# Masks for the diagonal blocks added by GpSimd instead of TensorE, no semaphore-clearing blocks between stages, and down-projection weights asked for earlier

## The reference

```python
z = rmsnorm(x) @ w_in                              # q, k, v, forget of group A; q, k, v of group B
# group A ("fox"), causal over the whole prompt; C = cumsum(log_sigmoid(forget))
s = q @ k.T * SCALE + (C[t] - C[s]); s = where(pos_s <= pos_t, s, -inf); o = softmax(s) @ v
# group B ("band"): own chunk of 64 and the 8 before it, with a learned bias by distance
# both groups once more for the streams, against their caches
x = x + rmsnorm(concat(rmsnorm(oA), rmsnorm(oB)) @ w_out)
h = rmsnorm(x)
x = x + rmsnorm((silu(h @ w_gate) * (h @ w_up)) @ w_down)
```

## Time and profile before

| what | value |
|---|---|
| median of 3 runs | 3088.11 us (3088.1 to 3093.4) |
| the profiled execution | 3088.66 us, span 3086.9 us |
| PE busy, share of the span | 2900.5 us, 94% |
| DVE, ACT, POOL busy | 1629.0, 1187.3, 631.5 us |
| mean granted TensorE clock | 0.977 of full speed |
| `attend` in the span | about 610 to 1325 us, its fox jobs to about 1005 |
| `mix_out`, `feed_forward` | from 1328.6 us, from 1591.7 us |
| last gate/up unit ends | about 2546.5 us |

### The profile page before, as it was taken

One profiled execution on the slowest core, in us unless ns is written; L12 is line 12 of the kernel. 1 busy time (PEld: TensorE's weight loads), 2 busy tenths in 40 slices (PEclk: granted clock), 3 DMA queues, 4 the chain that ended last, 5 costly groups with the idle time before them and its releaser, 6 DMA issues. The chain is left out here.

```text
span 3086.9 us, 57152 instructions
## 1 busy us (share of the span) xinstructions
PE 2900.5 (94%) x23073; PEld 2611.0 (85%) x23073; DVE 1629.0 (53%) x3168; ACT 1187.3 (38%) x2097; POOL 631.5 (20%) x544
## 2 busy tenths in 40 slices
PE   7999999889999889979959999999999998999998
PEld 7999999877778666758749999999999996887887
DVE  6222122176667567744456766776676663224443
ACT  5330000067767566644433334333433332223221
POOL 0000000032022123001134534453434330000000
PEclk9999999989999999989979999999999998999999
DMA  5322212142211886445623232333232425335553
GB/s 167 95 75 73 74 63 74 65 139 79 67 29 55 273 290 216 144 161 164 199 72 138 99 111 93 136 107 112 93 106 98 143 94 167 94 94 161 170 166 121
DMA packets 276157, 376.37 MB, mean 122 GB/s; under 512 B 16488, under 2 KB 203896, under 8 KB 263864
## 3 DMA queue, kind: packets, MB, share of 16 engines
q1 hardware_dynamic: 275608, 371.42, 37.5%
q10 hardware_dynamic: 288, 1.31, 0.1%
HBM read 283.52 MB, written 89.15 MB: 121 GB/s over the span
## 5 line engine op out<-in xcount | busy, mean ns | idle before, releaser
L1179 ACT ACTIVATE att_pts<-att_pt 128x384 f32<-128x384 f32 (+3 forms) x472 | 209.9, 483 | 224.0 <-PE att_pt L1065 209.5
L1168 ACT ACTIVATE att_sx<-att_sx,att_nm 128x640 f32<-128x640 f32 (+17 forms) x272 | 264.9, 980 | 9.4 <-DVE att_nm L1295 9.4
L79 PE MATMUL frt_pz<-frt_xhi,frt_hi 128*128 128x448 f32 (+1 forms) x640 | 230.5, 360 | 0.0
L81 PE MATMUL frt_pz<-frt_xhi,frt_lo 128*128 128x448 f32 (+1 forms) x640 | 230.5, 360 | 0.0
L80 PE MATMUL frt_pz<-frt_xlo,frt_hi 128*128 128x448 f32 (+1 forms) x640 | 230.0, 359 | 0.0
L514 DVE TENSOR_TENSOR frt_shared<-frt_pz,frt_rb 128x448 f32<-128x448 f32 (+1 forms) x80 | 48.9, 611 | 313.5 <-PE frt_pz L81 313.5
L1101 PE MATMUL att_po<-att_pts,att_vv 128*64 128x128 f32 x3296 | 212.1, 276 | 0.2 <-issue 0.2
L1065 PEld LDWEIGHTS att_pt<-att_eye,att_sx 64*128 64x128 f32 x3296 | 128.4, 139 | 98.5 <-ACT att_pts L1179 56.2
L1065 PE MATMUL att_pt<-att_eye,att_sx 64*128 64x64 f32 x3296 | 165.7, 232 | 46.1 <-ACT att_pts L1179 22.6
L1101 PEld LDWEIGHTS att_po<-att_pts,att_vv 128*64 128x64 f32 x3296 | 184.6, 138 | 11.3 <-ACT att_pts L1179 8.2
L79 PE MATMUL frt_pv<-frt_hi,frt_xhi 128*128 128x256 f32 (+1 forms) x544 | 157.4, 289 | 18.4 <-DVE frt_lo L446 15.5
(11 more groups left out here) (296 smaller groups left out, 8140.5 us busy)
## 6 DMA issues: line engine op xcount, KB each, us to landing
ahead_first<-mid_act SPq DMA_DIRECT2D x68, 704.0 KB, 6.7
ahead_second<-in_w_gu SPq DMA_DIRECT2D x33, 1024.0 KB, 5.1
ffn_wr<-in_w_gu SPq DMA_DIRECT2D x33, 1024.0 KB, 5.1
att_raw<-out_zT SPq DMA_DIRECT2D x64, 256.0 KB, 3.6
att_bb<-in_cache_ak SPq DMA_DIRECT2D x16, 1024.0 KB, 9.4
att_bb<-in_cache_av SPq DMA_DIRECT2D x16, 1024.0 KB, 10.0
mid_act<-ffn_ao SPq DMA_DIRECT2D x44, 362.0 KB, 2.4
out_zT<-frt_shared SPq DMA_DIRECT2D x64, 224.0 KB, 1.9
```

The source lines that it names most:

```text
L79: nc.tensor.matmul(out, a_hi(k), b_hi(k), start=(k == 0), stop=False)
L81: last = nc.tensor.matmul(out, a_lo(k), b_hi(k), start=False, stop=(k == kk - 1))
L1168: nc.scalar.activation(sx[n % NSX][:, e, :w], sx[n % NSX][:, e, :w], ACT.Exp, bias=nm[n % NSX][:, e:e + 1], scale=-1.0, accum_out=sums[n % ...
L1179: nc.scalar.activation(pts[G % NPT][:, :, 0:k, 64 * x:64 * x + 64], pt[x][:].rearrange("p (e j q) -> p e j q", e=2, q=64)[:, :, 0:k, :], A ...
```

## The change

1. **Mask.** The four matmuls on the diagonal and their operands go. `mask` (128 x 128) is made once. For each fox job POOL makes a masked copy of the bias of the last group: one TENSOR_TENSOR for the diagonal tile of both heads, and one COPY for the up to three tiles before it. It lies in a free part of `sx` or, from block 12 on, in a new buffer `mb`. DVE waits for it (`s_mk`) before the last group, and reads it instead of `bb`. POOL makes it three jobs ahead, for blocks 13 to 15 once DVE has evicted the job before. The stream masks move behind job 0's step in POOL's program, the band table to step 14.
2. **Start of attention.** The bias and the values of the first four tiles are asked for ahead of raw piece 2, the rest of both behind it.
3. **Clearing.** `mix_out` gets semaphores of its own, those of `feed_forward` are cleared by POOL within `mix_out`, behind its constants. Both clearing blocks go.
4. **Last gate/up unit.** Down blocks 8 to 11 are asked for a unit earlier, 12 to 15, the activations of tile 1, and 16 and 17 within the last unit. ACT splits the activations of tile 0 before the first eviction, and blocks up to 12 between evictions (6 before). DVE makes the low parts up to 10.

```diff
+                def masked(n):
+                    kind, p, i = JOBS[n]
...
+                    if 4 <= i < 12:
+                        pool.wait_ge(s_bi, 2 * S0[n - 2])
+                    if n == 12:
+                        pool.wait_ge(s_dc, 1)
+                    if i > 12:
+                        pool.wait_ge(s_bi, 2 * S0[n])
+                    nc.gpsimd.tensor_tensor(out[:, :, w - P:], bb[u][:, :, i * P:(i + 1) * P],
+                                            mask[:, None, :].to_broadcast([P, 2, P]), ALU.add).then_inc(s_mk, 1)
+                    if w > P:
+                        nc.gpsimd.tensor_copy(out[:, :, 0:w - P], bb[u][:, :, c0:c0 + w - P]).then_inc(s_mk, 1)
...
+                for n in range(3):
+                    masked(n)
                 for n in range(NJOB):
+                    if n == 1:
+                        stream_masks()
+                    if n == 14:
+                        band_table()
...
+                    if n + 3 < WIDE:
+                        masked(n + 3)
                     for x in splits_at(n):
                         split(x)
...
-                    if diag:
-                        for x in range(2):
-                            for e in range(2):
-                                r = slice(64 * e, 64 * e + 64)
-                                last = nc.tensor.matmul(S[e][k % 2][:, w - P:w], below[r, x, :], above[r, x, :], start=False,
-                                                        stop=(x == 1), skip_group_check=True)
...
+                    diag = fox(p) and tiles[-1] == i
+                    if diag:
+                        dve.wait_ge(s_mk, M0[n + 1])
                     for e in range(2):
-                        if fox(p):
+                        if diag:
+                            bias = masked_bias(n)[:, e, :]
+                        elif fox(p):
...
-                dve.wait_ge(s_pool, 8)
-                nc.vector.tensor_copy(below[:], ones[:])
-                nc.vector.tensor_copy(above[:], negs[:])
...
-                for x in range(NRAW):
+                for x in range(2):
                     load_raw(x)
-                load_bias(0)
-                load_v(0)
+                load_first(0, 4 * P, s_b0, s_v0)
+                for x in range(2, NRAW):
+                    load_raw(x)
+                load_first(4 * P, SEQ, s_b[0], s_v[0])
...
-        m.clear_sems()
         with nc.Block() as block:
...
+                for sem in later:
+                    pool.sem_clear(sem)
...
                     if n == NU - 2:
                         for q in range(4, 8):
                             down_weights(q)
-                    if n == NU - 1:
                         for sem in (l6, l3, l0):
                             sp.wait_ge(sem, NU - 1)
                         sp.wait_ge(s_t, 4 * (NU - 1))
                         for q in range(8, 12):
                             down_weights(q)
+                    if n == NU - 1:
+                        for q in range(12, 16):
+                            down_weights(q)
+                        acts(1)
+                        for q in range(16, 18):
+                            down_weights(q)
```

More of the change, by code:

```diff
@@ L661, in attend @@
     E0 = counted(1 if is_stream(n) else 2 for n in range(NJOB))
+    M0 = counted(min(len(job_groups(n)[-1]), 2) for n in range(NJOB) if JOBS[n][0] == "fox")
     ORDER = attend_order()
@@ L710, in attend @@
         eye = m.sb("eye", [P, P])
[L711 to L714, removed]
+        mask = m.sb("mask", [P, P])
+        mb = m.sb("mb", [P, 2, 4 * P])
         mine = m.sb("mine", [P, P])
@@ L1011, in score @@
                     q = slice(i * P, (i + 1) * P)
-                    diag = fox(p) and tiles[-1] == i
                     if p == 0 and i % 4 == 0:
@@ L1729, with up_sems, down_sems, feed_forward @@
 FFN_BYTES = AT_AO + 16 * max(w for _, w in TWIN)
-def feed_forward(nc, t, keep, ahead):
+def up_sems(m):
+    st = [m.sem(f"a_stored{u}") for u in range(2)]
+    l_w = [m.sem(f"weights{u}") for u in range(2)]
+    h0, ht, h3, h6, l0, lt, l3, l6 = (m.sem(f"w_{a}_{b}") for a in ("high", "low") for b in ("first", "sums", "lower", "up"))
+    (l_h, s_t, s_sp, s_sd, s_hh, s_hl, s_pr, s_p1, s_add, s_g1, s_g2, s_a) = (m.sem(n) for n in (
+        "h", "w_sums", "h_sums_pool", "h_sums_dve", "h_high", "h_low", "products", "first", "added",
+        "silu1", "silu2", "act"))
+    return (st, l_w, h0, ht, h3, h6, l0, lt, l3, l6, l_h, s_t, s_sp, s_sd, s_hh, s_hl, s_pr, s_p1, s_add, s_g1, s_g2, s_a)
+def down_sems(m):
+    l_d = [m.sem(f"down_weights{u}") for u in range(8)]
+    s_first = m.sem("first_high")
+    s_low = m.sem("a_low_pool")
+    l_x = [m.sem(f"x1{u}") for u in range(2)]
+    st_y = [m.sem(f"y_stored{u}") for u in range(2)]
+    (l_a, s_g, s_wh, s_wl, s_used, s_ah, s_al, s_y, s_ev, s_ss, s_vv, s_rr, s_sc, s_out, s_pw) = (m.sem(n) for n in (
+        "act_in", "gain", "down_high", "down_low", "down_used", "a_high", "a_low", "down_products", "evicted", "squares", "var", "rms",
+        "scaled", "out", "power"))
+    return (l_d, s_first, s_low, l_x, st_y, l_a, s_g, s_wh, s_wl, s_used, s_ah, s_al, s_y, s_ev, s_ss, s_vv, s_rr, s_sc, s_out, s_pw)
+def feed_forward(nc, t, up, down, ahead):
     HK = KD // 2
@@ L2183, in _ @@
                 up_done(act)
-                for j in range(7, NJ):
+                for j in range(13, NJ):
                     high_w(j)
```

208 lines of the change are left out of this document (118 added, 90 removed).

## The result

| | us |
|---|---|
| kernel before | 3088.11 (3087.74 to 3093.4, 4 runs) |
| changed kernel | 3073.63 (3071.28 to 3076.05, 4 runs) |
| ratio | 0.9949, 95% interval 0.9932 to 0.9966 |
| predicted | 3056, range 3046 to 3068 |

The changed kernel is 14.5 us faster, where 32 were predicted. The profiled execution took 3073.0 us (span 3071.3). The chip later ran it again, next to other kernels: 3071.5 against 3090.95 us, ratio 0.9934 (0.9922 to 0.9947). So the two sets give 14.5 and 19.5 us by their medians, about half of the 32 us predicted.

What follows compares the result with a forecast made beforehand. PE was taken to set the pace in the fox jobs (busy 89.0 of 95 us), with everyone waiting between stages. Terms: -15 + 0.5 + 0 - 1.8 - 7.3 - 8.5 = -32.1, from 3088.66 to 3056.6, as median 3056, range 3046 to 3068.

Steps and rivals of the forecast that it cites:

- The mask on TensorE: Fox jobs: removing 256 mask matmuls shortens PE's stream by 15 us, bounds -11 and -23.5.
- the 16 small ones: The four smallest fox jobs of each pair, where PE waits for a copy anyway; counted at 1 us.
- My bound of -11: Smallest gain allowed for removing the mask matmuls, if even some of the larger fox jobs wait.
- the fox jobs do not pay: Rival: PE's waits grow where the mask matmuls were; only 4 of the 15 us come, 3067; chance 0.08.
- The mask on GpSimd: Fox jobs: masks made by POOL cost 0, up to +4 if late; first pair's splits beside them +0.5.
- The start: Start of attention: first bias lands some 5.7 us sooner, but raw piece 3 is late next; 0, between -5.7 and +1.
- `brel`: Start of attention: its COPY moves to step 14 and no longer blocks a DVE split; -1.8, between 0 and -4.
- The clearing blocks: Between stages: SyncE's two waits of 7.3 us go in full, -7.3; the moved clears are hidden, 0 to +1.
- The last unit: Start of the down product: PE waits 4.1 instead of 11.5 us and resumes 8.1 sooner; -8.5, bounds -12 and -3.

## Why the prediction was wrong, point by point

- **The mask on TensorE, -15.** This is the step that failed: "64 x 0.29 = 18.6 us is what they take of PE's stream". Without them the kernel before is 4.2 us faster by the medians, 1 to 7 by the interval; by the fixed points it is 4.5 us in the three later pairs, and 2.1 to 3.4 in the first. Two things were wrong. The 0.29 us between the start of the four and the next start were taken as their price, without a look at the same step of a group that has no mask: 0.323 us stand between the last score pair and a turn of an output anyway, and the masked step of 0.498 is only 0.17 longer. And I let only "the 16 small ones" count for little. In 18 of the 44 masked groups whose step was measured a transposition follows, and for the 15 of these with 512 columns the step is as long without the mask. 26 x 0.17 = 4.4 us is the measured gain of the three later pairs. The reading of PE's waits looked at DVE's copies alone, and not at ACT's. My bound of -11 came from the same 0.29, so the range missed as well.
- **The rival "the fox jobs do not pay".** It had the right size (4 of 15 us), and only a small part of the mechanism: PE's waits grew by 0.6 us in the second pair. The rest of the missing 2.4 us a pair had never been in PE's stream.
- **The mask on GpSimd, 0 and +0.5.** Right in the later pairs, 93.9 us with and without. In the first pair it can't be told from the spread of that stretch. The rule that the prediction cites from the Trainium skill ("SBUF — State Buffer", Who interferes with whom) held: 0.75 us beside POOL.
- **The start, 0.** The cause was right, piece 3 decides, but I let it land when it did before. Its request left behind the rest of the bias on SyncE's queue, 2.6 us later than with the old order in the same kernel, and the piece landed 2.5 us later. The order costs about 3 us in the first pair, by the table below. The estimate of a bias 5.7 us sooner was 2 us.
- **`brel`, -1.8.** With the loads in the old order the changed kernel's first pair takes 122.6 us, and 124.8 in the kernel before without mask matmuls. In the 2.2 us between them stand the move of `brel`, the two casts on DVE that went with the masks' operands, and what POOL's masks cost. The term was not tried alone, and no run gives its size.
- **The clearing blocks, -7.3.** Measured 7.5.
- **The last unit, -8.5.** Sequence and place are right, the size is 7.0. Counted from the last unit's end, block 16 landed 1.65 us later than the 2552.5 forecast, so the gap is 5.9 us and not 4.1.

The first pair, from the end of `front` to its last output, in all profiled executions but that with the mask matmuls twice. Kernels whose first pair is the same differ by up to 2.2 us:

| first pair | us |
|---|---|
| before; with the clearing alone, with the last unit alone changed | 128.3, 126.9, 127.8 |
| before, without mask matmuls | 124.8 |
| changed kernel, twice; with tile 1's low part on DVE; the attention's change alone | 126.1, 124.1, 125.9, 126.2 |
| changed kernel without GpSimd's masks | 124.4 |
| changed kernel with the old load order, twice | 122.6, 122.4 |
| changed kernel with raw piece 3 early, twice | 122.9, 121.8 |

The new order (125.6 in the mean) costs about 3 us against the old one and against piece 3 early (122.5 and 122.4), and its quickest execution (124.1) is slower than the slowest of those (122.9). The second and third pair repeat to 0.04 us in every kernel with the same work on PE.

Together, by the fixed points: -4.5 in the three later pairs, -2.1 in the first pair as a whole (128.3 to 126.1), and -7.5 and -7.0 from the two parts tried alone. That is -21.1 against -32.1. Of the 11 us between them 6.8 are the mask matmuls in the later pairs (three quarters of 15 were forecast), 2.9 the first pair (-5.0 was forecast: a quarter of 15, +0.5 and -1.8) and 1.5 the last unit, less 0.2 at the clearing. The second set's 19.5 us agree. The profiled execution shows 5 us less: its `front` ended 2.0 us later in unchanged code, and its band jobs took 1.9 us longer, with 7.4 us at the lower clock instead of 4.6. What brings those falls of the clock about stays open.

## What to carry to other kernels

The price of an instruction in a busy engine's stream is the step with it less the step without it. A trace often holds both, here in masked and unmasked groups a few microseconds apart. The time from its start to the next start also holds what the next instruction costs in any case, and its busy time counts overlaps. Where a load is put ahead of others, ask when each request behind it leaves the queue, not only in which order the bytes move. A gain of 3 us in one stretch of one execution has to be held against the spread of that stretch. Where two engines block one another, giving the work to one of them can be faster than sharing it: 3.1 us in line on DVE in place of 6.1 us on POOL, with DVE standing.

## What the runs showed of the hardware

- A group of four 64 x 128 x 128 matmuls in two row halves took 0.17 us of PE's stream before a 128-row matmul, nothing before a transposition that would have waited, and 0.22 us when it was the second such group.
- With both inputs in SBUF, DVE stood while POOL subtracted: three blocks took 7.49 us beside POOL's 6.14, and four took 2.5 us without it. DVE's evictions from PSUM took 0.75 us beside a POOL subtraction.
- A smaller DMA did not land in proportion. Of the bias, spread over 128 partitions by two DMAs, 2 x 256 KB came 7.2 us behind raw piece 0, and before the change 2 x 1024 KB came 9.2 us behind it. In 616 to 618 the DMA engines were busy to 0.80 and moved 84 GB/s; before, in the same stretch, to 1.00 with 377 GB/s.
- Executions of one kernel differ by short drops of the granted clock that come and go at the same places of the program. In 1143 to 1153 the changed kernel had 0.83 in its first profiled execution and 1.00 in its second, behind the same wait of PE of 1.79 us:

```profile
1143.00:1153.00 10.00, 7.67 (x107) 6.35 (x105) 4.82 (x19) 3.63 (x8) 3.46 (x5) 0.83 1.04 291
```

```profile
1143.00:1153.00 10.00, 8.04 (x136) 5.98 (x132) 5.83 (x24) 4.94 (x12) 3.96 (x6) 1.00 1.03 296
```

The waits of PE, in the same order:

```profile
1147.77 0.60 PE L1102 MATMUL att_pt<-att_eye,att_sx 64*128 64x64 f32 x8 [1.79 <-issue]
```

```profile
1148.35 0.46 PE L1102 MATMUL att_pt<-att_eye,att_sx 64*128 64x64 f32 x8 [1.79 <-issue]
```

The kernel before ran from 3081.68 to 3097.8 in 32 executions; how much of that such drops make is not shown. It is why gains of 3 us were read in stretches between fixed points and not from the whole.
